# Two projections of a second block as pairs of 64-row products, with the halves added by DVE

## What is computed

```python
def hybrid_layer(x, mem, pre_g, post_g, w_in, ...):
    hn = rmsnorm(x, pre_g)
    proj = hn @ w_in                       # 1024 -> 6664
    (ret_q, ret_k, ret_v, ret_g, xbc, z, dt_raw,
     sb_q, sb_k, sb_v, sb_g, mem_q, mem_g) = split(proj)
    y_ret = retention(ret_q, ret_k, ret_v) * silu(ret_g)
    y_ssd = ssd_mixer(xbc, z, dt_raw, ...)
    y_sb = stick_breaking(sb_q, sb_k, sb_v) * silu(sb_g)
    y_mem = memory_read(mem_q, ...) * silu(mem_g)
    y = concatenate([y_ret, y_ssd, y_sb, y_mem]) @ w_out
    return x + rmsnorm(y, post_g)
```

## Time and profile before

| | |
|---|---|
| median of 3 runs | 2046.41 us (2045.88 to 2047.19) |
| the profiled execution | 2047.67 us, of which the span of the trace is 2045.9 |
| PE busy | 2034.8 us (99%) |
| DVE busy | 901.1 us (44%) |
| ACT busy | 670.3 us (33%) |
| second block | about 1555 to 2044 us of the span |

### The profile page before, as it was taken

One profiled execution on the slowest core, in us unless ns is written; L12 is line 12 of the kernel. 1 busy time (PEld: TensorE's weight loads), 2 busy tenths in 40 slices (PEclk: granted clock), 3 DMA queues, 4 the chain that ended last, 5 costly groups with the idle time before them and its releaser, 6 DMA issues.

```text
span 2045.9 us, 39090 instructions
## 1 busy us (share of the span) xinstructions
PE 2034.8 (99%) x17579; PEld 1356.0 (66%) x17579; DVE 901.1 (44%) x1251; ACT 670.3 (33%) x896; POOL 46.6 (2%) x69
## 2 busy tenths in 40 slices
PE   9999999999999999999999999999999999999998
PEld 6888888888889353434434353535347888888887
DVE  6777554467776100101010101010126777677775
ACT  5575543455755100000000000000005645456452
POOL 4100000000000000000000000000000000000000
PEclk9999999999999999999999999999999999999999
DMA  9654565554546999999999999999997544465342
GB/s 319 157 184 155 205 209 189 189 180 152 199 160 228 408 419 411 403 420 403 420 398 419 403 419 394 420 403 420 410 404 270 181 146 150 155 203 181 128 165 84
DMA packets 160048, 570.81 MB, mean 279 GB/s; under 512 B 13209, under 2 KB 26273, under 8 KB 128898
## 3 DMA queue, kind: packets, MB, share of 16 engines
q1 hardware_dynamic: 151040, 546.74, 70.7%
q0 software_dynamic: 5280, 17.16, 2.6%
q10 hardware_dynamic: 3554, 4.33, 0.6%
HBM read 562.80 MB, written 5.39 MB: 278 GB/s over the span
## 4 chain that ended last, share of the span: by engine, by line
PE 98%; DMA 1%; DVE 0%; ACT 0%; DVEq 0%; issue 0%; POOL 0%; SPq 0%; ACTq 0%; POOLq 0%
PE bank L1045 40%; PE bank L1400 28%; PE bank L1432 13%; PE bank L1100 5%; PE bank L1107 3%; PE bank L1118 2%; PE bank L1051 1%; DMA ring<-moe_w_down 1%; PE bank L1144 0%; PE bank L1657 0%; PE bank L1664 0%; PE bank L1665 0%; PE bank L1685 0%; PE bank L1671 0%; PE bank L1663 0%; PE bank L1154 0%
## 5 line engine op out<-in xcount | busy, mean ns | idle before, releaser
L1045 PE MATMUL bank<-halves_r,x_both 128*128 128x512 f32 x2624 | 607.8, 390 | 0.0
L1400 PE MATMUL bank<-ring,xT 128*32 128x512 f32 (+1 forms) x6144 | 580.4, 539 | 0.0
L1045 PEld LDWEIGHTS bank<-halves_r,x_both 128*128 128x128 f32 x2624 | 489.9, 188 | 101.7 <-issue 1.5
L1400 PEld LDWEIGHTS bank<-ring,xT 128*32 128x32 f32 x6144 | 198.8, 110 | 372.9 <-issue 371.4
L2618 DVE TENSOR_TENSOR halves_r<-ring,halves_r 128x2048 fp32r<-128x2048 f32 x170 | 384.0, 2287 | 132.7 <-ACT halves_r L2045 131.1
L2045 ACT ACTIVATE halves_r<-ring 128x2048 fp32r<-128x2048 f32 x172 | 325.1, 1914 | 187.9 <-DMA ring<-w_in 74.6
L3147 DVE TENSOR_TENSOR arena<-arena,bank 128x512 f32<-128x512 f32 (+1 forms) x48 | 29.8, 620 | 727.6 <-PE bank L1400 726.2
L1432 PE MATMUL bank<-ring,arena 128*32 128x256 f32 x5376 | 293.4, 379 | 0.9 <-DMA ring<-moe_w_down 0.7
L1432 PEld LDWEIGHTS bank<-ring,arena 128*32 128x32 f32 x5376 | 175.7, 110 | 116.4 <-issue 5.4
L2232 ACT ACTIVATE arena<-bank 128x512 f32<-128x512 f32 (+1 forms) x58 | 32.1, 553 | 460.8 <-PE bank L1400 428.5
L1100 PE MATMUL bank<-x_both,halves_r 128*128 128x512 f32 x448 | 107.3, 392 | 0.3 <-DVE x_both L3433 0.3
(11 more groups left out here) (412 smaller groups left out, 1551.7 us busy)
## 6 DMA issues: line engine op xcount, KB each, us to landing
ring<-moe_w_gate_up SPq DMA_DIRECT2D x128, 1024.0 KB
ring<-moe_w_down SPq DMA_DIRECT2D x112, 1024.0 KB
ring<-w_in SPq DMA_DIRECT2D x99, 1024.0 KB, 5.1
ring<-moe_w_gate_up SPq DMA_DIRECT2D x128, 768.0 KB
ring<-w_out SPq DMA_DIRECT2D x24, 1024.0 KB, 4.9
ring<-ffn_w_gate_up SPq DMA_DIRECT2D x20, 1024.0 KB, 5.2
ring<-ffn_w_down SPq DMA_DIRECT2D x11, 1024.0 KB, 4.9
ring<-w_in SPq DMA_DIRECT2D x18, 512.0 KB, 6.1
```

What stands on the lines that cost most here:

```text
L1045: return pe.matmul(o[:, a:a + n], x[:, c, b * P:(b + 1) * P], w[:, k, col:col + n], **flags)
L1400: mm = pe.matmul(shaped(o[i][GROUP * z:GROUP * (z + 1), 0:u], u // P, P), xg[:, c, GROUP * i:GROUP * (i + 1)], w[:, q, z, :, :], start=c == 0,
```

## The change

In each layer of the second block, SV and RV no longer go through `by_rows`, but through `by_half_rows`. Each product of 128 rows becomes two of 64 rows: rows 0 to 63 of the activations and weights go into the bank of SV0 (SV1, RV0, RV1), rows 64 to 127 into a second bank, a new job UV0 (UV1, TV0, TV1). All four banks are taken at the start of the projection. ACT copies the first banks out as before. DVE gets `add_lower_rows`, which adds the second bank to the copied block and frees it: for SV after the split of RQ, for RV after the split of O1. The four new jobs stand in the list of jobs, which moves the banks of those after them, and PE's readers wait for UV1 and TV1.

```diff
-    "... PY1 AR2 SV0 SV1 "
+    "... PY1 AR2 SV0 UV0 SV1 UV1 "
...
-    "RV0 RV1 PS2 TS3 ..."
+    "RV0 TV0 RV1 TV1 PS2 TS3 ..."
...
+        job = {"SV1": "UV1", "RV1": "TV1"}.get(job, job)
...
+                def by_half_rows(name, jobs):
+                    tile = (name, l)
+                    for h in halves(tile):
+                        half, over = (tile, h), h == halves(tile)[-1]
+                        cs = list(enumerate(half_chunks(tile, h)))
+                        if h == 0:
+                            outs = [[begin(job, l) for job in pair] for pair in jobs]
+                        def product(b, part, x, w, c, k, **flags):
+                            s = slice(part * P // 2, (part + 1) * P // 2)
+                            return pe.matmul(outs[b][part][:, :], x[s, c, b * P:(b + 1) * P], w[s, k, :], **flags)
+                        w = high_half(half)
+                        for b in range(TB):
+                            for k, c in cs:
+                                for x in (xT_high, xT_low):
+                                    for part in range(2):
+                                        mm = product(b, part, x, w, c, k, start=c == 0 and x is xT_high, stop=False)
+                        mm.then_inc(top_free[tops.slot(half)], 1)
+                        w = low_half(half)
+                        for b in range(TB):
+                            for k, c in cs:
+                                for part in range(2):
+                                    mm = product(b, part, xT_high, w, c, k, start=False, stop=c == KC - 1)
+                                    if c == KC - 1:
+                                        mm.then_inc(*end(jobs[b][part], l))
+                        if not over:
+                            mm.then_inc(*raw_end(half))
...
-                by_rows("SV", ["SV0", "SV1"])
+                by_half_rows("SV", [("SV0", "UV0"), ("SV1", "UV1")])
...
-                pe.wait_ge(*drained("SV1", l))
+                pe.wait_ge(*drained("UV1", l))
...
-                by_rows("RV", ["RV0", "RV1"])
+                by_half_rows("RV", [("RV0", "TV0"), ("RV1", "TV1")])
...
-                pe.wait_ge(*drained("RV1", l))
+                pe.wait_ge(*drained("TV1", l))
...
+                def add_lower_rows(dst, job, other):
+                    for b in range(TB):
+                        dve.wait_ge(*drained(f"{job}{b}", l))
+                        dve.wait_ge(*full(f"{other}{b}", l))
+                        dve.tensor_tensor(dst[:, b, :], dst[:, b, :], out_of(f"{other}{b}")[:, :],
+                                          ALU.add).then_inc(*fr(f"{other}{b}"))
...
                 split(("RQ", l))
+                add_lower_rows(v2, "SV", "UV")
                 stick_softplus(0)
...
                 split(("O1", l))
+                add_lower_rows(vm, "RV", "TV")
                 stick_out(3)
```

## The result

The kernel with the change takes 2096.43 us, median of 5 runs (2093.78 to 2098.12), against 2046.41 (2045.88 to 2047.19): 1.0238 times as long, 95% interval 1.0227 to 1.0249. The forecast was 2094. The profiled execution is the one of 2096.43, with a span of 2094.6; the sum had its own time at 2095.4.

What follows compares the result with a forecast made beforehand. PE was taken as the bound, busy 99% of the span. The profiled 2047.67 + 36.5 (waits) + 1.2 (form) + 10 (clock) gave 2095.4, or 2094 in terms of the runs' median; range 2079 to 2108 us.

Steps and rivals of the forecast that it cites:

- SG on UV0: Ahead of SG in each layer, PE waits until DVE's add, behind RQ's split, frees UV0: 7.5 us.
- RV on PS1: Ahead of RV in each layer, PE waits until DVE's stick_out(1) frees PS1: 4.9 us.
- wait 1: PE's wait ahead of SG for UV0's bank, 7.5 us a layer; said to buy the wait ahead of RV nothing.
- RG on TV0: Ahead of RG in each layer, PE waits until DVE's add, behind O1's split, frees TV0: 5.85 us.
- The pair at the price of a whole product: In SV and RV, two 64-row products cost one whole product, 228 ns; bounds 2.9 us gained, 43.8 us lost.
- In and out of the form: PE entering and leaving the 64-row form around SV and RV: 0.3 us, four times, 1.2 us; bounds 0 and 2.4.
- The clock: PE's clock drops after standing still, slowing work behind six waits: 10 us taken, bounds 0 and 22, at most 3.7 each.
- waits 2 and 3: PE's waits ahead of RV for PS1, 4.9 us, and ahead of RG for TV0, 5.85 us, in each layer.
- The rival in which the clock holds: PE's clock stays up through the waits, leaving 37.7 us of loss: 2084 us, chance 0.16.
- The rival of pairs one after the other: In SV and RV, a pair's products run in turn, each projection 11 us longer: 2138 us, chance 0.07.
- DVE finds time: Ahead of RV, the wait shrinks as DVE drops work that SG's wait let it do early: 2081 us, chance 0.07.
- Not slower: Banks are free when PE comes, as adds run ahead of RQ's and O1's splits: 2045 to 2048 us, chance 0.03.

Runs made afterwards that it cites:

- the filled version: Kernel with the change, but PE issues 30, 19 and 20 products of unused result while waiting ahead of SG, RV and RG: 2084.01 us, 1.0179.
- the version of 2048.94: Kernel with the change, but all adds moved earlier, second banks of RV and RG taken later, stick_out(1) put ahead of rotate RK1: 2048.94 us, 1.0009.

## Why the prediction was right

The point at which it was decided was not the product but the list of banks. Counting eight places back in the list gave three jobs whose bank was freed late, and those three are the ones that PE idles at, to 0.3 us in size, in both layers, and at no other. Taking a bank later or freeing it earlier took each wait away, and all three together took 47 of 50 us.

*SG on UV0*: 7.5 forecast, 7.44 measured. The add started where the old record had the next instruction, and lasted 0.68 as the rotation's first product does.

*RV on PS1*: 4.9 forecast, 5.09 measured. RV starts 0.25 us behind the end of `stick_out(1)`, where SG and RG start 0.1 or less behind an add's. The rest of that is probably the entry to the 64-row form, 0.17 where no wait stands ahead of it, which the sum had as a term of its own; no run separates the two. That wait 1 would not pay for it was argued from DVE's chain; the kernel with SV's adds moved shows it, with wait 2 unchanged.

*RG on TV0*: 5.85 forecast, 5.58 measured. Two small things make the difference. Leaving the 64-row form brings PE to RG 0.2 us later behind the end of RV's record than the forecast had it, so less of DVE's chain is left to wait for. And ACT's copy of RV1 starts where that record ends (1742.37 against 1742.33), as forecast, but the rounding of O1 starts 0.1 before the copy's record ends (1742.86 against 1742.97). From there to RG it is 7.1 us, as forecast.

*The pair at the price of a whole product*: 227 ns, right, and both bounds wrong: the 14 ns by which a whole rounded product is longer than the 213 ns of the lower bound stay in the pair. The estimate from the Trainium skill's 60 cycles a matmul (TensorEngine Tiling (Array Packing), Instruction Overhead), 4.8 us more, is not borne out: with the waits gone, 192 extra products and all four changes of form cost 1.6 us by the rows and 1.95 in the median (0 to 3.7).

*In and out of the form*: 1.2 forecast, 1.6 measured, 0.4 a projection and not 0.3.

*The clock*: 10 forecast, 12.0 measured from the rows and 11.4 to 13.3 given back in the filled version. The mechanism was right. The size was a choice between 0 and 22, so that it came within 2 us is in part luck; it was too low because I doubted that waits 2 and 3, some 5 us long, bring the clock down; all six waits did. The slow stretches behind the waits cost 1.5 to 2.9 us each, not the 3.7 of the upper bound. The rival in which the clock holds is what the filled version made: 2084.01 measured, 36.7 above the kernel before in the same runs, against 2084 and 37.7 in the forecast. The rival of pairs one after the other has its price measured too, 42 to 44.

*DVE finds time* did not happen. *Not slower* needed more than the adds ahead of the splits: `stick_out(1)` had to move too, and banks had to be taken later. That is the version of 2048.94, and there it is no change, as that rival's arithmetic had it (2045 to 2048), a microsecond above its upper end. The lower end of the stated range comes to 2078 by its own terms and not 2079; nothing hangs on it.

What stays open: no row tells why the clock stayed down longer behind the same wait in one layer than in the other (last section). And 2048.94 is 1.95 above the kernel before in the median, where the rows explain 1.6; the interval, 0 to 3.7 us, includes both.

## What to carry to other kernels

When buffers are handed out in turn from a list, a new entry changes who waits for whom for eight places behind it. Write down for each of them who frees its buffer now and where that instruction stands in its engine's order; the new work itself may cost next to nothing (here 1.6 us) while the places cost 48. On an engine that never idled, price a wait twice: its length, and what the clock costs behind it. A product split over the array's rows is free in time, but for the change of form, if its parts alternate; it gains nothing if the whole array was in use before.

## What the runs showed of the chip

Products on different rows of the array ran side by side even when they were issued in turns of eight, at 1.8 us a projection more than in alternation (13.05 against 11.22 for the records of SV), and 5.5 more in turns of sixteen (16.74). The starts of the records fit a product of the idle rows that begins four places ahead of its turn; the records do not name the rows, so this is a reading. That products do not start strictly in the order of the program rests on the totals alone. If products started in order, only the last of a turn and the first of the next could run together. SV has 16 turns in the first kernel (4 times 8, 8, 4, 4), so 96 - 15 = 81 steps of 227 ns, 18.4 us; 8 turns in the second, 89 steps, 20.2 us. The Trainium skill has matmuls start and end in program order (TensorE: Matmul & The Clock Gate, Part 3, on packing small matmuls); the totals of these two runs do not agree with it, unless the products reached PE in another order than the program's, which no run here tests.

A slow stretch stood behind all six waits of 5.1 to 7.4 us, in one of them (RV in layer 1) with a clock that fell only as the work began. What it cost differed between layers for the same wait: SG lost 2.89 us in layer 0 and 1.63 in layer 1, with the same 7.44 us ahead of it. In layer 0 the clock was at 0.50 for the first 5.9 us of SG; in layer 1 its mean over the first 5.1 us is 0.69, which makes some 3.2 us at 0.50. Half of each is what SG lost. Why the two differ, no run here shows.
